# Retention gates evacuated without Silu into four buffers; Silu in place once the last head's exponentials are done, the gating products behind it

## The chip, the cores and the metric

The kernel runs on 1 core of one Trainium2 chip. The metric is the device time of one execution in microseconds (us), the median over several runs; smaller is better. A profiled execution gives the rows that are read here. Engines are called by their names or by the profile's: PE is TensorE (PEld its weight load), DVE VectorE, ACT ScalarE, POOL GpSimd, SP SyncE.

## The reference, cut to what matters

A model of three blocks on 256 tokens of width 1024: a differential attention and an mLSTM, each followed by a squared-ReLU MLP, and then a hybrid layer with a retention branch, a multi-head latent attention (MLA) branch, a third MLP and a gated embedding. The change is in the hybrid layer's two branches, which are computed side by side:

```python
h = rms_norm(x, norm_mix)
rq, rk, rv, rg, cq, ckv, krope, gr, gm = jnp.split(h @ w_in, offsets, axis=-1)
...
ro = retention(rq, rk, rv)                       # 4 heads of 512
ro = rms_norm(ro, ret_norm)
a_ret = (ro * jax.nn.silu(rg)) @ w_br            # rg: the retention gates, 2048 wide
...
s = q @ k * scale                                # MLA, 8 heads
s = jnp.where(causal, s, -1e30)
mo = jax.nn.softmax(s, axis=-1) @ v
a_mla = mo @ w_bm
mixed = jax.nn.sigmoid(gr) * a_ret + jax.nn.sigmoid(gm) * a_mla
```

## The kernel before, in words

**Weights in units.** Every product with a weight matrix is a `dense` group of 512 output columns. Its weights come in units of 128x1024 floats (512 KB) through a ring of 8: SyncE loads `raw`, ScalarE copies it, rounded, to `w_hi` (line 1190), VectorE subtracts it to get the rest, `w_lo` (line 1625), and TensorE makes three products for each pair of operands (lines 697 to 699). ScalarE and VectorE work 6 units ahead of TensorE. When TensorE has used a unit, `unit_used` counts up and the next load can start.

**Groups and banks.** The groups alternate between two pairs of PSUM banks, `pair0` and `pair1`. When a group is done ScalarE evacuates it (`empty`, line 1235), scaled by the rows' norm; the group after the next needs that evacuation. The order on every engine is written out by hand; the program's blocks for each engine list the groups in the same order, and the dictionary given to `dense` says what is done behind which unit of a group ("slot"). Nothing is reordered: an engine that waits holds everything behind it.

**The stretch of the change.** The groups `rv0` to `rv3` are the retention's values, with the retention's own products `ret0` to `ret3` between; `rg0` to `rg3` are the gates, and behind them come `gm0`, `gm1`, `gr0`, `gr1` (sigmoid gates) and `br0`, `br1`. Within `rg1` to `rg3` the slots run the MLA heads as a pipeline, `mla_slot(n)` behind one unit each: slots 0 to 3 in `rg1`, 4 to 7 in `rg2`, 8 and 9 behind the first two units of `rg3`. In slot n TensorE makes the scores of head n, the value product of head n-2 (lines 1079 to 1081), and the transpositions of head n-1's probabilities (line 725, out of `l_work`), which need that head's exponentials. VectorE masks the scores and takes the maxima (lines 2158 and 2161); ScalarE makes the exponentials (line 1494), copies the transposed probabilities back (line 1500) and scales head n-2's output (line 1507).

**The gates.** ScalarE evacuates gate group n with Silu into one of two buffers, `work[n % 2]`, which the retention's values used earlier. `gate_out(n)` on VectorE multiplies the retention's output, its norm factor and the gate (line 2096), two products of 128x512. `roT.0` to `roT.14` are the transpositions of that result in slots of `gm0` and `gm1`: ScalarE and VectorE split each into `b_hi` (line 1205) and `b_lo` (line 1643); `roT.0` and `roT.2` need product 0, `roT.4` and `roT.6` product 1, and so on.

**Tables.** Exp, Silu and Sigmoid are evaluated from different tables here. Where an activation needs another table than the one that is active, an ACT_TABLE_LOAD stands before it in the program, at the line of that activation. Copy and Square never have one.

Of the kernel before, what the change touches and what calls it, by code (L numbers as in the profile page):

```python
# [12 lines left out]
ALU = mybir.AluOpType  # L13
ACT = mybir.ActivationFunctionType
# [4 lines left out]
TT = S // P  # L19
# [3 lines left out]
HALF = 512  # L23
# [249 lines left out]
def build(nc, w, out):  # L273
    groups, group_list, stream, mlps = schedule(w)
# [4 lines left out]
    with ExitStack() as ctx:  # L279
        def sb(name, shape, dt=F32, scope=ctx):  # L280
            return scope.enter_context(nc.sbuf_tensor(name, [P, *shape], dt))

        def sem(name):
            return ctx.enter_context(nc.semaphore(name))
# [105 lines left out]
        ph = ctx  # L390
# [3 lines left out]
        work = sb("work", [2, TT, HALF], scope=ph)  # L394
# [30 lines left out]
        with ExitStack() as ph:  # L425
            kv = sb("kv", [TT, MLA_H, NOPE + P], scope=ph)
            lq_n = sb("lq_n", [MLA_H, S], scope=ph)
            lq_t = sb("lq_t", [MLA_H // 2, S], scope=ph)
            lk_n = sb("lk_n", [MLA_H, S], scope=ph)
            lk_t = sb("lk_t", [MLA_H // 2, S], scope=ph)  # L430
            l_work = sb("l_work", [2048], scope=ph)
        lk_flat = lk_n[:, :, :].rearrange("p h s -> p (h s)")
        rot = l_work[:, 0:TT * MLA_H * ROPE].rearrange("p (t h d) -> p t h d", t=TT, h=MLA_H)
        prod = l_work[:, 1024:2048].rearrange("p (t h d) -> p t h d", t=TT, h=MLA_H)
        l_e = l_work[:, 0:2 * SCORE].rearrange("p (b n) -> p b n", b=2)
        l_pt = l_work[:, 2 * SCORE:4 * SCORE].rearrange("p (b n) -> p b n", b=2)
        with ExitStack() as ph:
# [17 lines left out]
        group_act = sem("group_act")  # L455
# [70 lines left out]
        ret_out = sem("ret_out")  # L526
# [9 lines left out]
        l_exped = sem("l_exped")  # L536
        l_reced = sem("l_reced")
        gated = sem("gated")
        mixed = sem("mixed")
        p_loaded = sem("p_loaded")  # L540
        out_ready = sem("out_ready")
# [30 lines left out]
        def wait_group(eng, name):  # L572

            eng.wait_ge(unit_used, groups[name]["units"][-1][0] + 1)

        def group_ps(name):
            return pair[groups[name]["index"] % 2]
# [32 lines left out]
        def run_group(name, each, slots=None, part=slice(None)):  # L610

            for n, unit in list(enumerate(groups[name]["units"]))[part]:
                each(unit)
                if slots and n in slots:
                    slots[n]()
# [553 lines left out]
        def _(act):  # L1169
# [22 lines left out]
            def split_until(k):  # L1192

                while split_to[0] <= min(k, total_units - 1):
                    split_unit(split_to[0])
                    split_to[0] += 1

            def split_turn(name):

                wait_turn(act, name)  # L1200
                for src, hi, _, scale in split_parts(name):
                    if scale is None:
                        act.activation(hi, src, ACT.Copy).then_inc(turn_act, 1)
                    else:
                        act.activation(hi, src, ACT.Copy, scale=scale).then_inc(turn_act, 1)
# [16 lines left out]
            def dense(name, slots=None, part=slice(None), ahead=AHEAD):  # L1222

                run_group(name, lambda u: split_until(u[0] + ahead), slots, part)

            def empty(name, outs, func=ACT.Copy, scales=None):

                wait_group(act, name)
                for tt in range(TT):
                    ps = group_ps(name)[:, tt, 0:groups[name]["ncols"]]  # L1230
                    ps = ps if len(outs[tt].shape) == 2 else ps.rearrange("p (a b) -> p a b", a=outs[tt].shape[1])
                    if scales is None:
                        act.activation(outs[tt], ps, func).then_inc(group_act, 1)
                    else:
                        act.activation(outs[tt], ps, func, scale=scales[tt]).then_inc(group_act, 1)  # L1235

            def row_norm(v):
                return [rstd[:, v, tt:tt + 1] for tt in range(TT)]
# [251 lines left out]
            def mla_exp(h):  # L1490
                act.wait_ge(l_maxed, h + 1)
                b = h % 2
                for j, cols in enumerate((WIDE, TALL)):
                    last = act.activation(l_e[:, b, cols], l_e[:, b, cols], ACT.Exp, bias=l_nm[:, b, j:j + 1],
                                          accum_out=l_sum[:, b, j:j + 1])
                last.then_inc(l_exped, 1)

            def mla_probs(h):
                wait_turn(act, f"lp{h}")
                act.activation(l_pt[:, h % 2, :], turn_bank(f"lp{h}")[:, 0:SCORE], ACT.Copy).then_inc(turn_act, 1)  # L1500

            def mla_value(h):

                wait_turn(act, f"lv{h}")
                act.wait_ge(l_reced, h + 1)
                for tt in range(TT):
                    act.activation(lo_sb[:, tt, h * P:(h + 1) * P], turn_bank(f"lv{h}")[:, tt * P:(tt + 1) * P],
                                   ACT.Copy, scale=l_rec[:, h % 2, 1 - tt:2 - tt]).then_inc(turn_act, 1)

            def mla_slot(n):  # L1510
                if 1 <= n <= MLA_H:
                    mla_exp(n - 1)
                if n >= 2:
                    mla_value(n - 2)
                if 1 <= n <= MLA_H:
                    mla_probs(n - 1)
# [26 lines left out]
                    wait_turn(act, "rk1b")  # L1543
                empty(f"rv{n}", [work[:, n % 2, tt, :] for tt in range(TT)], scales=row_norm(5))

            def empty_gate(n):

                act.wait_ge(ret_out, 3 if n == 0 else 4)
                if n >= 2:
                    act.wait_ge(gated, n - 1)  # L1550
                empty(f"rg{n}", [work[:, n % 2, tt, :] for tt in range(TT)], ACT.Silu, row_norm(5))

            dense("rv0")
            empty_value(0)
# [9 lines left out]
            ret_squares(2)  # L1564
            dense("rg0")
            empty_gate(0)
            ret_squares(3)
            dense("rg1", {n: (lambda n=n: mla_slot(n)) for n in range(4)})
            empty_gate(1)
            dense("rg2", {n: (lambda n=n: mla_slot(4 + n)) for n in range(4)})  # L1570
            empty_gate(2)
            dense("rg3", {0: lambda: mla_slot(8), 1: lambda: mla_slot(9)})
            empty_gate(3)
            dense("gm0", {n: (lambda n=n: split_turn(f"roT.{2 * n}")) for n in range(4)})
            empty("gm0", [gm[:, tt, 0:HALF] for tt in range(TT)], ACT.Sigmoid, row_norm(5))
            dense("gm1", {n: (lambda n=n: split_turn(f"roT.{8 + 2 * n}")) for n in range(4)})
# [39 lines left out]
        def _(dve):  # L1616
# [11 lines left out]
            def split_until(k):  # L1628
                while split_to[0] <= min(k, total_units - 1):
                    split_unit(split_to[0])  # L1630
                    split_to[0] += 1

            def dense(name, slots=None, part=slice(None), ahead=AHEAD):
                run_group(name, lambda u: split_until(u[0] + ahead), slots, part)

            def split_turn(name):

                dve.wait_ge(turn_act, turn[name]["act_end"])
                for src, hi, lo, scale in split_parts(name):
                    if scale is None:  # L1640
                        dve.tensor_tensor(lo, src, hi, ALU.subtract).then_inc(turn_dve, 1)  # L1641
                    else:
                        dve.scalar_tensor_tensor(lo, src, scale, hi.bitcast(F32), ALU.mult, ALU.subtract)\
                            .then_inc(turn_dve, 1)
# [444 lines left out]
            def gate_out(n):  # L2089

                dve.wait_ge(ret_norm, 1)
                dve.wait_ge(group_act, groups[f"rg{n}"]["act_end"])
                dve.wait_ge(group_dve, groups["ret3"]["dve_end"])
                cols = slice(n * HALF, (n + 1) * HALF)
                for tt in range(TT):
                    last = dve.scalar_tensor_tensor(ret[:, tt, cols], ret[:, tt, cols], ret_r[:, tt, n:n + 1],
                                                    work[:, n % 2, tt, :], ALU.mult, ALU.mult)
                last.then_inc(gated, 1)

            def mla_sums_q():  # L2100
# [69 lines left out]
            def mla_slot(n):  # L2170
                if n < MLA_H:
                    mla_logits(n)
                if 1 <= n <= MLA_H:
                    mla_recip(n - 1)
# [31 lines left out]
            dense("rg0", {n: (lambda n=n: mla_rot_copy("mk", n)) for n in range(2)})  # L2206
            ret_value(3)
            dense("rg1", {n: (lambda n=n: mla_slot(n)) for n in range(4)})
            gate_out(0)
            dense("rg2", {n: (lambda n=n: mla_slot(4 + n)) for n in range(4)})  # L2210
            gate_out(1)
            dense("rg3", {0: lambda: mla_slot(8)})
            gate_out(2)
            gate_out(3)
            dense("gm0", {n: (lambda n=n: split_turn(f"roT.{2 * n}")) for n in range(4)})
            dense("gm1", {n: (lambda n=n: split_turn(f"roT.{8 + 2 * n}")) for n in range(4)})
            dense("gr0")
            dense("gr1")
# [209 lines left out]
```

## Time and profile before

| | |
|---|---|
| time of the runs | 1213.6, 1214.57, 1215.23 us; median 1214.57 |
| the profiled execution's own time | 1209.92 us |
| its span, first to last instruction | 1208.1 us |
| mean granted TensorE clock | 0.993 |
| TensorE busy | 1170.8 us, 97% |
| TensorE weight load busy | 965.5 us, 80% |
| VectorE busy | 748.1 us, 62% |
| ScalarE busy | 628.5 us, 52% |
| DMA, mean | 170 GB/s |

The profile shows one execution. A row of a timeline is one instruction (or several of one kind, "x2", merged): its start in us from the span's start, its length in us, the engine, the line, the operation, what it writes and reads, and in brackets how long its engine stood idle before it and for whom. Matmuls are pipelined: one shown as 0.39 us long is followed by the next 0.23 us after its start, so starts are to be compared, not ends.

### The profile page before, as it was taken

Reading aid. Unit: us, or ns where it says so; the run is one execution under the profiler, and the core shown is the slowest. Engines: PE = TensorE matmul, PEld = TensorE weight load, DVE = VectorE, ACT = ScalarE, POOL = GpSimd, SP = SyncE. Lnnn points to the kernel's source line nnn. Section 1 sums busy time; section 2 is a strip of 40 time slices with the busy share of each in tenths; the row PEclk is TensorE's granted clock in tenths of the full one; section 3 lists DMA queues with packets and bytes.
Section 4 is the critical chain, followed back from the end, with each engine's and each line's share of the span. In section 5 each row is a group of like instructions: output and inputs, shape, how many; then the busy total and the mean of one; then the engine's idle time right before and its main releaser. Section 6 shows DMA issues by size and latency. Waiting matters only on the chain.

```text
span 1208.1 us, 15885 instructions
## 1 busy us (share of the span) xinstructions
PE 1170.8 (97%) x5722; PEld 965.5 (80%) x5722; DVE 748.1 (62%) x1003; ACT 628.5 (52%) x970; POOL 63.5 (5%) x77
## 2 busy tenths in 40 slices
PE   6999999999999999999989999998999999999997
PEld 4778788888878878888877887777888877888886
DVE  4687656646585665656568778444645666556564
ACT  5587545435457654435455455565744454444443
POOL 2001000000000100000030042000000000000000
PEclk9999999999999999999999999999999999999999
DMA  8743455555456455555565555423665645555542
GB/s 248 257 145 122 156 177 190 191 191 189 143 141 172 150 181 191 188 182 187 168 190 182 168 162 157 139 88 88 174 182 184 190 150 176 190 191 191 191 160 85
DMA packets 95122, 205.60 MB, mean 170 GB/s; under 512 B 7805, under 2 KB 10149, under 8 KB 95072
## 3 DMA queue, kind: packets, MB, share of 16 engines
q1 hardware_dynamic: 93216, 199.61, 51.9%
q0 software_dynamic: 1696, 5.26, 1.5%
q8 instruction: 30, 0.49, 0.2%
q14 instruction: 20, 0.16, 0.0%
q10 hardware_dynamic: 160, 0.07, 0.0%
HBM read 203.86 MB, written 2.63 MB: 171 GB/s over the span
## 4 chain that ended last, share of the span: by engine, by line
PE 89%; DVE 3%; DMA 3%; ACT 3%; SPq 1%; issue 1%; POOL 0%; ACTq 0%
PE pair L697 16%; PE pair L699 16%; PE pair L698 16%; PE turn_ps L794 7%; PE pair L794 7%; PE turn_ps L796 4%; PE score L699 4%; PE score L697 4%; PE score L698 4%; PE pair L796 4%; PE turn_ps L725 3%; DMA raw<-in_w_in 1%; DVE w_lo L1625 1%; DMA raw<-in_attn_w_in 1%; SPq L644 1%
## 5 line engine op out<-in xcount | busy, mean ns | idle before, releaser
L1625 DVE TENSOR_TENSOR w_lo<-raw,w_hi 128x1024 fp32r<-128x1024 f32 (+2 forms) x381 | 457.6, 1224 | 199.5 <-ACT w_hi L1190 193.9
L1190 ACT ACTIVATE w_hi<-raw 128x1024 fp32r<-128x1024 f32 (+2 forms) x381 | 391.4, 1048 | 229.1 <-DMA raw<-in_mlp_w 63.2
L697 PE MATMUL pair<-w_hi,a_both 128*128 128x512 f32 (+3 forms) x560 | 226.1, 404 | 5.1 <-ACT lat_sb L1235 4.1
L699 PE MATMUL pair<-w_hi,a_both 128*128 128x512 f32 (+3 forms) x560 | 217.1, 388 | 0.0
L698 PE MATMUL pair<-w_lo,a_both 128*128 128x512 f32 (+3 forms) x560 | 216.5, 387 | 0.0
L794 PE MATMUL pair<-a_both,w_hi 128*128 128x512 f32 x384 | 143.5, 398 | 1.6 <-DVE up_sum L1671 1.6
L794 PE MATMUL turn_ps<-a_both,w_hi 128*128 128x512 f32 x384 | 142.6, 396 | 2.0 <-DVE p_lo L1641 2.0
L697 PEld LDWEIGHTS pair<-w_hi,a_both 128*128 128x128 f32 x560 | 107.1, 191 | 28.8 <-ACT lat_sb L1235 4.4
L699 PEld LDWEIGHTS pair<-w_hi,a_both 128*128 128x128 f32 x560 | 106.7, 191 | 21.8
L698 PEld LDWEIGHTS pair<-w_lo,a_both 128*128 128x128 f32 x560 | 107.3, 192 | 19.9 <-issue 1.2
L796 PE MATMUL pair<-a_both,w_lo 128*128 128x256 f32 x384 | 107.6, 280 | 0.0
L796 PE MATMUL turn_ps<-a_both,w_lo 128*128 128x256 f32 x384 | 107.5, 280 | 0.0
L1671 DVE TENSOR_TENSOR up_sum<-pair,up_low 128x512 f32<-128x512 f32 x24 | 16.6, 691 | 125.2 <-ACT up_low L1254 125.2
L794 PEld LDWEIGHTS pair<-a_both,w_hi 128*128 128x128 f32 x384 | 72.1, 188 | 20.5 <-DVE up_sum L1671 3.1
L794 PEld LDWEIGHTS turn_ps<-a_both,w_hi 128*128 128x128 f32 x384 | 72.0, 188 | 19.5 <-DVE p_lo L1641 2.3
L1254 ACT ACTIVATE up_low<-pair 128x512 f32<-128x512 f32 x24 | 14.3, 596 | 139.1 <-PE turn_ps L796 139.1
L796 PEld LDWEIGHTS pair<-a_both,w_lo 128*128 128x128 f32 x384 | 72.5, 189 | 0.9
L796 PEld LDWEIGHTS turn_ps<-a_both,w_lo 128*128 128x128 f32 x384 | 72.5, 189 | 0.0
L699 PE MATMUL score<-w_hi,h_lo 128*128 128x512 f32 x168 | 65.8, 392 | 0.0
L697 PE MATMUL pair<-w_hi,h_hi 128*128 128x512 f32 x168 | 65.8, 392 | 0.0
L699 PE MATMUL pair<-w_hi,h_lo 128*128 128x512 f32 x168 | 65.8, 392 | 0.0
L697 PE MATMUL score<-w_hi,h_hi 128*128 128x512 f32 x168 | 65.8, 391 | 0.0
(358 smaller groups left out, 1629.5 us busy)
## 6 DMA issues: line engine op xcount, KB each, us to landing
raw<-in_mlp_w SPq DMA_DIRECT2D x128, 512.0 KB, 3.3
raw<-in_w_in SPq DMA_DIRECT2D x64, 512.0 KB, 3.7
raw<-in_w_up SPq DMA_DIRECT2D x32, 512.0 KB, 3.5
raw<-in_w_down SPq DMA_DIRECT2D x32, 512.0 KB, 3.2
raw<-in_attn_w_in SPq DMA_DIRECT2D x24, 512.0 KB, 7.0
raw<-in_mlstm_w_in SPq DMA_DIRECT2D x24, 512.0 KB, 3.8
raw<-in_w_br SPq DMA_DIRECT2D x16, 512.0 KB, 3.7
raw<-in_attn_w_out SPq DMA_DIRECT2D x8, 512.0 KB, 3.7
```

The source lines that it names most:

```text
L644: sp.dma_start(dst, src).then_inc(landed[k % RING], 16)
L697: pe.matmul(o, hi, whi, start=start, stop=False)
L698: pe.matmul(o, hi, wlo, start=False, stop=False)
L699: return pe.matmul(o, lo, whi, start=False, stop=stop)
L725: last = pe.transpose(bank[:, j * P:(j + 1) * P], src, ident)
L794: pe.matmul(ups[i][:, b, :], w_hi[:, slot, cols], a_both[:, c, :, :], start=c == 0, stop=False)
L796: last = pe.matmul(ups[i][:, b, S:], w_lo[:, slot, cols], a_hi[:, c, :], start=False, stop=c == DC - 1)
L1190: act.activation(w_hi[:, k % RING, 0:n], raw[:, k % RING, 0:n], ACT.Copy).then_inc(hi_ready, 1)
L1254: act.activation(up_low[:, 2 * i:2 * i + 2, :], ups[i][:, :, S:], ACT.Copy).then_inc(up_copied, 1)
L1625: dve.tensor_tensor(w_lo[:, k % RING, 0:n], raw[:, k % RING, 0:n], w_hi[:, k % RING, 0:n], ALU.subtract).then_inc(lo_ready, 1)
L1671: dve.tensor_tensor(up_sum[:, 2 * i:2 * i + 2, :], ups[i][:, :, 0:S], up_low[:, 2 * i:2 * i + 2, :], ALU.add)\
```

## The change

The gate groups are evacuated by Copy in place of Silu, except the last, and into four buffers: a new tile `gate_raw` holds gates 0 and 1, `work` gates 2 and 3. Silu is then applied in place by a new function `silu_gate`: for gate 0 behind the third unit of `rg3`, for gate 1 behind the fourth, for gate 2 behind the group; head 7's exponentials are over by then. `gate_out` waits for a new semaphore `gate_silu`. On VectorE the products for gates 0 and 1 move from behind `rg1` and `rg2` to slots 2 and 3 of `rg3`, those for gates 2 and 3 from behind `rg3` to slots 0 and 1 of `gm0`, each behind the split of a transposition. The evacuations of gates 0 and 1 no longer wait for `ret_out`, the one of gate 2 waits for `ret_out` of 3 in place of 4, and none waits for `gated`.

```diff
@@ tiles, semaphores
+            gate_raw = sb("gate_raw", [2, TT, HALF], scope=ph)
+        gates = [gate_raw[:, n, :, :] for n in range(2)] + [work[:, n, :, :] for n in range(2)]
+        gate_silu = sem("gate_silu")
@@ ScalarE
-            def empty_gate(n):
-
-                act.wait_ge(ret_out, 3 if n == 0 else 4)
+            def empty_gate(n, func=ACT.Copy):
+
                 if n >= 2:
-                    act.wait_ge(gated, n - 1)
-                empty(f"rg{n}", [work[:, n % 2, tt, :] for tt in range(TT)], ACT.Silu, row_norm(5))
+                    act.wait_ge(ret_out, n + 1)
+                empty(f"rg{n}", [gates[n][:, tt, :] for tt in range(TT)], func, row_norm(5))
+
+            def silu_gate(n):
+
+                act.wait_ge(group_act, groups[f"rg{n}"]["act_end"])
+                act.activation(gates[n], gates[n], ACT.Silu).then_inc(gate_silu, 1)
@@
             empty_gate(2)
-            dense("rg3", {0: lambda: mla_slot(8), 1: lambda: mla_slot(9)})
-            empty_gate(3)
+            dense("rg3", {0: lambda: mla_slot(8), 1: lambda: mla_slot(9), 2: lambda: silu_gate(0),
+                          3: lambda: silu_gate(1)})
+            silu_gate(2)
+            empty_gate(3, ACT.Silu)
@@ VectorE
                 dve.wait_ge(ret_norm, 1)
-                dve.wait_ge(group_act, groups[f"rg{n}"]["act_end"])
+                if n < 3:
+                    dve.wait_ge(gate_silu, n + 1)
+                else:
+                    dve.wait_ge(group_act, groups["rg3"]["act_end"])
...
                     last = dve.scalar_tensor_tensor(ret[:, tt, cols], ret[:, tt, cols], ret_r[:, tt, n:n + 1],
-                                                    work[:, n % 2, tt, :], ALU.mult, ALU.mult)
+                                                    gates[n][:, tt, :], ALU.mult, ALU.mult)
@@
             dense("rg1", {n: (lambda n=n: mla_slot(n)) for n in range(4)})
-            gate_out(0)
             dense("rg2", {n: (lambda n=n: mla_slot(4 + n)) for n in range(4)})
-            gate_out(1)
-            dense("rg3", {0: lambda: mla_slot(8)})
-            gate_out(2)
-            gate_out(3)
-            dense("gm0", {n: (lambda n=n: split_turn(f"roT.{2 * n}")) for n in range(4)})
+            dense("rg3", {0: lambda: mla_slot(8), 2: lambda: gate_out(0), 3: lambda: gate_out(1)})
+            dense("gm0", {0: lambda: (split_turn("roT.0"), gate_out(2)), 1: lambda: (split_turn("roT.2"), gate_out(3)),
+                          2: lambda: split_turn("roT.4"), 3: lambda: split_turn("roT.6")})
```

The first place is ScalarE at the end of `rg1` (slot 3 ends with the copy to `l_work`). `l_work` of line 1494 is head 3's exponentials, `w_hi` the weight half six units ahead; behind "waits" stand the semaphores. Before:

```order
L1500 ACTIVATE l_work<-turn_ps 128x384 [waits turn_filled]
L1235 ACT_TABLE_LOAD [waits unit_used]
L1235 ACTIVATE work<-pair,rstd 128x512 [waits ret_out]
L1235 ACTIVATE work<-pair,rstd 128x512
L1190 ACTIVATE w_hi<-raw 128x1024 [waits landed1,unit_used]
L1494 ACT_TABLE_LOAD
L1494 ACTIVATE l_work,l_sum<-l_work,l_nm 128x256 [waits l_maxed]
L1494 ACTIVATE l_work,l_sum<-l_work,l_nm 128x128
```

The same place in the changed kernel, whose lines have moved down by three:

```order
L1503 ACTIVATE l_work<-turn_ps 128x384 [waits turn_filled]
L1238 ACTIVATE gate_raw<-pair,rstd 128x512 [waits unit_used]
L1238 ACTIVATE gate_raw<-pair,rstd 128x512
L1193 ACTIVATE w_hi<-raw 128x1024 [waits landed1,unit_used]
L1497 ACTIVATE l_work,l_sum<-l_work,l_nm 128x256 [waits l_maxed]
L1497 ACTIVATE l_work,l_sum<-l_work,l_nm 128x128
```

Both table loads are gone. It is the same at the end of `rg2`; at `rg0` the load ahead of the evacuation is gone, and the one ahead of head 0's exponentials is still there.

The second place is ScalarE in `rg3`, from the second to last weight half of the group on. Before:

```order
L1190 ACTIVATE w_hi<-raw 128x1024 [waits landed7,unit_used]
L1190 ACTIVATE w_hi<-raw 128x1024 [waits landed0,unit_used]
L1235 ACT_TABLE_LOAD [waits unit_used,gated]
L1235 ACTIVATE work<-pair,rstd 128x512 [waits ret_out]
L1235 ACTIVATE work<-pair,rstd 128x512
L1190 ACTIVATE w_hi<-raw 128x1024 [waits landed1,unit_used]
```

And in the changed kernel:

```order
L1193 ACTIVATE w_hi<-raw 128x1024 [waits landed7,unit_used]
L1558 ACT_TABLE_LOAD
L1558 ACTIVATE gate_raw<-gate_raw 128x1024 [waits group_act]
L1193 ACTIVATE w_hi<-raw 128x1024 [waits landed0,unit_used]
L1558 ACTIVATE gate_raw<-gate_raw 128x1024 [waits group_act]
L1558 ACTIVATE work<-work 128x1024 [waits group_act]
L1238 ACTIVATE work<-pair,rstd 128x512 [waits unit_used,ret_out]
L1238 ACTIVATE work<-pair,rstd 128x512
L1193 ACTIVATE w_hi<-raw 128x1024 [waits landed1,unit_used]
```

The table load has moved ahead by one weight half, and three Silus in place have come in.

The third place is VectorE from the last head's reciprocal to the splits in `gm0` (`ret` is the product of `gate_out`, `b_lo` the split of a transposition). Before:

```order
L2168 RECIPROCAL l_rec<-l_sum 128x2 [waits turn_act,l_exped]
L1625 TENSOR_TENSOR w_lo<-raw,w_hi 128x1024 [waits hi_ready] x3
L2096 SCALAR_TENSOR_TENSOR ret<-ret,ret_r,work 128x512 [waits group_dve,group_act,ret_norm]
L2096 SCALAR_TENSOR_TENSOR ret<-ret,ret_r,work 128x512
L2096 SCALAR_TENSOR_TENSOR ret<-ret,ret_r,work 128x512 [waits group_dve,group_act,ret_norm]
L2096 SCALAR_TENSOR_TENSOR ret<-ret,ret_r,work 128x512
L1625 TENSOR_TENSOR w_lo<-raw,w_hi 128x1024 [waits hi_ready]
L1643 SCALAR_TENSOR_TENSOR b_lo<-turn_ps,gains,b_hi 128x256 [waits turn_act]
```

And in the changed kernel:

```order
L2180 RECIPROCAL l_rec<-l_sum 128x2 [waits turn_act,l_exped]
L1634 TENSOR_TENSOR w_lo<-raw,w_hi 128x1024 [waits hi_ready] x2
L2108 SCALAR_TENSOR_TENSOR ret<-ret,ret_r,gate_raw 128x512 [waits group_dve,gate_silu,ret_norm]
L2108 SCALAR_TENSOR_TENSOR ret<-ret,ret_r,gate_raw 128x512
L1634 TENSOR_TENSOR w_lo<-raw,w_hi 128x1024 [waits hi_ready]
L2108 SCALAR_TENSOR_TENSOR ret<-ret,ret_r,gate_raw 128x512 [waits group_dve,gate_silu,ret_norm]
L2108 SCALAR_TENSOR_TENSOR ret<-ret,ret_r,gate_raw 128x512
L1634 TENSOR_TENSOR w_lo<-raw,w_hi 128x1024 [waits hi_ready]
L1652 SCALAR_TENSOR_TENSOR b_lo<-turn_ps,gains,b_hi 128x256 [waits turn_act]
L1652 SCALAR_TENSOR_TENSOR b_lo<-turn_ps,gains,b_hi 128x256
L2108 SCALAR_TENSOR_TENSOR ret<-ret,ret_r,work 128x512 [waits group_dve,gate_silu,ret_norm]
L2108 SCALAR_TENSOR_TENSOR ret<-ret,ret_r,work 128x512
```

Products 0 and 1, formerly in the MLA's slots, now stand in `rg3` a weight half apart, product 2 behind the first `b_lo`, and product 3, not shown, behind the second.

## Rows read from the trace of the kernel before

**Rows 1.** The page: the span, and TensorE's busy time, share and instructions.

```profile
span 1208.1 us, 15885 instructions
PE 1170.8 (97%) x5722; PEld 965.5 (80%) x5722; DVE 748.1 (62%) x1003; ACT 628.5 (52%) x970; POOL 63.5 (5%) x77
```

**Rows 2.** Waits of PE, 0 to 850 us: total us, times, longest us.

```profile
PE turn_ps L725 <- ACT l_work L1494: 4.3, 2, 3.2
```

**Rows 3.** Waits of PE from 850 us on, the first of four.

```profile
PE turn_ps L794 <- DVE p_lo L1641: 2.0, 1, 2.0
...
```

**Rows 4.** Timeline of PE, 804 to 818 us (slots 3 and 4).

```profile
...
806.14 0.39 PE L1081 MATMUL turn_ps<-kv,l_work 128*128 128x128 f32 x2
806.36 0.49 PE L725 MATMUL turn_ps<-square,l_work 128*128 128x128 f32 x3
...
811.97 0.39 PE L1081 MATMUL turn_ps<-kv,l_work 128*128 128x128 f32 x2
813.44 0.55 PE L725 MATMUL turn_ps<-square,l_work 128*128 128x128 f32 x3 [1.08 <-ACT l_work L1494]
...
```

**Rows 5.** Timeline of PE, 829 to 866 us (slot 8).

```profile
...
834.54 0.39 PE L1081 MATMUL turn_ps<-kv,l_work 128*128 128x128 f32 x2
838.10 0.55 PE L725 MATMUL turn_ps<-square,l_work 128*128 128x128 f32 x3 [3.17 <-ACT l_work L1494]
...
```

**Rows 6.** Timeline of PE behind `ret2` and behind `ret3`.

```profile
...
769.34 1.02 PE L1045 MATMUL pair<-work,ret_s 128*128 128x512 f32 x2
...
770.44 0.39 PE L698 MATMUL pair<-w_lo,a_both 128*128 128x512 f32 x1
...
783.81 1.02 PE L1045 MATMUL pair<-work,ret_s 128*128 128x512 f32 x2
...
785.29 0.40 PE L698 MATMUL pair<-w_lo,a_both 128*128 128x512 f32 x1
...
```

**Rows 7.** Timeline of ACT around the evacuations of `rg1` and `rg2`.

```profile
...
795.59 1.05 ACT L1190 ACTIVATE w_hi<-raw 128x1024 fp32r<-128x1024 f32 x1
796.53 0.50 ACT L1494 ACTIVATE l_work<-l_work,l_nm 128x256 f32<-128x256 f32 x1
...
807.59 1.28 ACT L1235 ACT_TABLE_LOAD   x1
...
810.04 1.05 ACT L1190 ACTIVATE w_hi<-raw 128x1024 fp32r<-128x1024 f32 x1
...
812.40 0.51 ACT L1494 ACTIVATE l_work<-l_work,l_nm 128x256 f32<-128x256 f32 x1
...
837.06 0.51 ACT L1494 ACTIVATE l_work<-l_work,l_nm 128x256 f32<-128x256 f32 x1
...
```

**Rows 8.** Table loads of ACT by line, 740 to 1000 us: busy us, mean ns.

```profile
L1235 ACT ACT_TABLE_LOAD x5 | 6.4, 1283 | 2.7 <-PE pair L699 2.6
...
L1494 ACT ACT_TABLE_LOAD x3 | 3.8, 1283 | 0.1
...
```

**Rows 9.** Timeline of DVE: head 7's maxima, and the products of gate 2.

```profile
...
830.95 0.61 DVE L2161 TENSOR_REDUCE l_nm<-l_work 128x1 f32<-128x256 f32 x2
...
847.39 1.41 DVE L2096 SCALAR_TENSOR_TENSOR ret<-ret,ret_r,work 128x512 f32<-128x512 f32 x2
...
```

**Rows 10.** Line 1411, the mLSTM's Silu in place: duration in ns, min/median/max.

```profile
L1411 ACT ACTIVATE ml_t<-ml_t x4: 617/620/632, 368.4 to 373.0; 128x512 f32<-128x512 f32 x4
```

**Rows 11.** Timeline of ACT in the second half of `rg3`.

```profile
...
842.64 1.06 ACT L1190 ACTIVATE w_hi<-raw 128x1024 fp32r<-128x1024 f32 x1
845.16 1.06 ACT L1190 ACTIVATE w_hi<-raw 128x1024 fp32r<-128x1024 f32 x1 [1.46 <-DMA raw<-in_w_in]
847.64 1.28 ACT L1235 ACT_TABLE_LOAD   x1 [1.43 <-PE pair L699]
...
```

**Rows 12.** Timeline of PE: the transpositions of `roT.0`.

```profile
...
850.11 0.60 PE L725 MATMUL turn_ps<-square,ret 128*128 128x128 f32 x4
...
```

**Rows 13.** Busy us (instructions) of each engine in 850 to 870 us; TensorE clock, DMA.

```profile
850.00:870.00 20.00, 20.00 (x103) 16.46 (x102) 14.64 (x21) 14.21 (x23) 0.00 (x0) 1.00 0.57 170
```

## The prediction

> **What bounds the kernel now.** I read the page first. TensorE has 1170.8 us of work in a span of 1208.1 us [rows 1], so the kernel is bound by TensorE's stream, and a change elsewhere is worth only what it takes out of TensorE's gaps, 37 us in all. Then I read TensorE's own waits. In the stretch with the gates the largest is 4.3 us in two pieces, the longer 3.2 us: the transpositions of line 725 waiting for the exponentials of line 1494 on ScalarE [rows 2]. The same query behind 850 us gives four waits, the longest of 2.0 us in the last MLP, and none of them is for a weight half (`w_hi`, `w_lo`) [rows 3]. So behind the gates TensorE is not short of weights, and microseconds won before stay won.
>
> Third, TensorE's timeline. In an undisturbed slot (slot 3) the last value product of line 1081 starts at 806.14 and the transpositions follow 0.22 us later. In slot 4 they start 1.47 us after line 1081 (811.97 to 813.44), in slot 8 3.56 us after it (834.54 to 838.10) [rows 4, 5]. Above the undisturbed 0.22 us the excess is **1.25 us** in slot 4 and **3.34 us** in slot 8. A third and smaller gap lies behind `ret3`: from the last line 1045 to the first line 698 of `rg1` there are 1.48 us (783.81 to 785.29), where the same place behind `ret2`, whose evacuation had no table load, took 1.10 us (769.34 to 770.44) [rows 6]. The excess is **0.38 us**.
>
> Fourth, ScalarE's timeline says why. At 807.59 it begins to evacuate `rg1`: a table load for Silu, two activations, a weight half at 810.04, another load, and only at 812.40 the exponential of head 3, for which TensorE's transpositions of slot 4 stand waiting [rows 7]. The same sequence for `rg2` ends with the exponential of head 7 at 837.06, and the transpositions of slot 8 start 1.04 us later [rows 5, 7].
>
> **What the change removes.** ScalarE's order of before has eight table loads in this stretch (five of line 1235, three of line 1494, each 1283 ns) [rows 8]. In the changed order `rg0` to `rg2` are evacuated by Copy, in whatever table is there (the `w_hi` copies between exponentials already run so), and three loads are left: for head 0's exponential, for the first Silu, for `gm0`'s Sigmoid. Five go.
>
> What a load costs ScalarE is read from two pairs. Weight half to exponential without a load: 795.59 to 796.53, 0.94 us. With one: 810.04 to 812.40, 2.36 us [rows 7]. The difference is 1.42 us: the load, and the overlap of 0.13 us that back-to-back activations have and a load breaks. The page "ScalarE: Activation LUTs" of the Trainium skill, section "What ACT_TABLE_LOAD costs", gives about 1.28 us for the load and about 1.38 us more for a drain, 2.66 us a switch. This trace agrees with the load and not with the drain; by the page's figure the slot 8 gap would vanish wholly, and the sum below would be 5.0 instead of 4.5 us.
>
> Now each gap:
> - `rg1` (behind `ret3`): its first matmul needs `rg0` evacuated. The load at the head of that evacuation goes, 1.42 us against a lateness of 0.38 us. All of it goes: **0.38 us**.
> - Slot 4: two loads ahead of the exponential of head 3, 2.84 us, against an excess of 1.25 us. The exponential would start at 812.40 − 2.84 = 809.56 and be over some 1.6 us before TensorE has finished line 1081. All goes: **1.25 us**.
> - Slot 8: two loads ahead of the exponential of head 7, which would start at 837.06 − 2.84 = 834.22. Is it ready by then? Its maxima on VectorE start at 830.95 and last 0.61 us, so yes [rows 9]. The transpositions follow 1.04 us behind, at 835.26, where TensorE could take them at 834.76. Of 3.34 us **2.84 us** go and 0.50 us stay, since the evacuation of `rg2` and the weight half still stand ahead of the exponential.
>
> Sum: 0.38 + 1.25 + 2.84 = 4.47, **4.5 us**.
>
> **What it adds.** Three Silus in place of 128x1024 on ScalarE. The nearest row is the Silu in place of 128x512 at 617 to 632 ns [rows 10]; the `w_hi` copy of 128x1024, a double width, takes 1.06 us [rows 11]. I take 1.05 us each, 3.2 us together (bounds: 0.62 us if width cost nothing, 1.26 us for twice the narrow row). They lie where ScalarE has room. In the frame of before: weight half at 842.64 for 1.06 us, then idle 1.46 us to the next at 845.16, and idle 1.43 us again until TensorE finishes `rg3` and the load starts at 847.64 [rows 11]. With the change: load 843.7 to 845.0, Silu 0 to 846.05, weight half to 847.0, Silu 1 to 848.0, Silu 2 to 849.0, then `rg3`'s evacuation. Before, that evacuation's activations started behind their load, at 847.64 + 1.28 = 848.9. So the three Silus cost nothing there; without that cover they would cost ScalarE 3.2 us, and even so `rg3`'s pair of banks is next wanted by `gm1`, four units later.
>
> **Where the new wait goes.** `gate_out(0)` now waits for Silu 0 and its two products take 1.41 us [rows 9]: done at about 847.6. TensorE wants it at 850.11, for `roT.0` [rows 12]: 2.5 us of slack. Queued behind it on VectorE is one `w_lo`, for a unit six ahead. Products 2 and 3 go in between the `b_lo` splits of `gm0`. VectorE is busy 14.64 of 20 us there, the last product of before included [rows 13]; one pair more leaves about 4 us idle, and products 2 and 3 are wanted by `roT.8` and `roT.12`, units later. Taking the two products out of slots 4 and 7 frees VectorE 2.8 us, which nobody waited for. Nothing is issued anew on the DMA queues, and no step is moved past one. The removed waits on `gated` and `ret_out` had been met long before.
>
> **From the profile to the median.** The sum is made in the profiled execution, 1209.92 us with its 1208.1 us span. The median of the runs is 1214.57 us, 4.65 us above that; the gaps are waits between engines, so I take 4.5 us off each: 1205.4 us for a profiled execution like this one, 1210.1 us for the median, 0.37% less.
>
> **The rivals.**
> - *Forecast: the three gaps shrink as computed.* 1210.1 us, own range 1209.3 to 1211.2 (a spread of the runs of ±0.8 us; the slot 8 term between one load's 1.42 and the whole 3.34 us). Chance 0.72.
> - *The whole slot 8 gap goes.* That needs the two loads to hold the chain for 3.34 us, 1.67 us each, against 1.42 us by my pair. It gives 0.38 + 1.25 + 3.34 = 4.97, 1209.6 us. This is how it would come out by the page's 2.66 us a switch. Chance 0.08.
> - *Another wait takes the place in slot 8*, the longer gap: the weight half between `rg2`'s evacuation and the exponential then waits for its transfer or its ring slot, which the loads hide today. Only 1.63 us are won, 1212.9 us, within 0.2%. Against it: in the row of before that half starts without idle time, and its unit's slot has been free for units. The same number comes if some of the gain is given back later, against which stand the rows behind 850 us [rows 3]. Chance 0.15.
> - *Slower: TensorE waits at `roT.0` for product 0.* Place: between the first and second unit of `gm0`. Price: each microsecond by which the product ends more than 2.5 us after my 847.6. The kernel is slower than before once it is 2.5 + 4.5 = 7.0 us late, and by over 0.2% from 9.4 us. At 12 us late it is 1210.1 + 9.5 = 1219.6 us. Three Silus of 1.05 us can't do that; they would have to take some 4 us each, or Silu 0 would have to be held by a weight half that arrives late. Chance 0.05.
>
> **How the numbers follow.** A change of 0.2%, 2.4 us, is about what a measurement of this kernel can tell from none. The first two cases are faster by more (0.80, of which I give 0.02 to the spread of the runs, and take 0.03 from the third case, where half the slot 8 term may come): faster 0.81. Same: 0.14. Slower: 0.05. The range reaches from under the second case, 1209.6 less the spread of 0.8 (1208.8, taken to 1208.5), to the third, 1212.9.
>
> **What would show it.** In the changed kernel's trace: three table loads between 770 and 865 us where there were eight; slot 4's transpositions directly behind line 1081 (0.22 us); slot 8's 0.7 us behind it, TensorE's wait for the exponentials down from 4.3 to about 0.5 us; no wait of TensorE for `ret` ahead of `roT.0`; three Silus of about 1.05 us in `rg3`, the first product done some 2.5 us before TensorE's transposition. The prediction is wrong if a wait for `w_lo`, for a turn's bank or for `ret` stands in TensorE's list, or if the exponential of head 7 still starts more than 3 us behind the start of `rg2`'s evacuation.

## The result, and the profile after

The changed kernel took **1206.93 us** (median of 20 runs, 1202.99 to 1212.3). The kernel before took 1212.66 us (20 runs, 1209.68 to 1218.45; the three runs behind the 1214.57 us in the table above are among them). The medians are 5.7 us apart; the ratio is 0.9949, 95% interval 0.9935 to 0.9963, which is 6.2 us faster (4.5 to 7.9). Faster was forecast; the time forecast, 1210.1 us, is 3.2 us too high, and 1206.93 lies below the range of 1208.5 to 1212.9.

The profiled execution of the changed kernel is one of the longest of the 20, 1211.89 us. Its span is longer than the span before (mean granted clock 0.989 against 0.993, and a long wait near the start), so here the two totals say nothing. The page, and TensorE's waits from 0 to 850 us (total us, times, longest us):

```profile
span 1210.1 us, 15878 instructions
PE 1175.0 (97%) x5719; PEld 970.4 (80%) x5722; DVE 747.7 (62%) x1003; ACT 624.5 (52%) x968; POOL 63.4 (5%) x77
```

```profile
...
PE score L904 <- DVE da_e L1812: 4.7, 1, 4.7
...
PE turn_ps L728 <- ACT l_work L1497: 0.3, 1, 0.3
```

The 4.7 us are a wait in the first block, far from the change, for an operation that TensorE did not wait for in the execution of before; the last experiment comes back to it. The wait for the exponentials has gone from 4.3 us to 0.3 [rows 2]. Of the eight table loads between 740 and 1000 us [rows 8] three are left, as forecast:

```profile
...
L1497 ACT ACT_TABLE_LOAD x1 | 1.3, 1283 | 0.0
L1558 ACT ACT_TABLE_LOAD x1 | 1.3, 1283 | 0.0
L1238 ACT ACT_TABLE_LOAD x1 | 1.3, 1283 | 0.0
```

TensorE's timeline of the changed kernel answers to [rows 4 to 6] and [rows 12] (line numbers are higher by three):

```profile
...
776.01 1.02 PE L1048 MATMUL pair<-work,ret_s 128*128 128x512 f32 x2
...
777.11 0.39 PE L701 MATMUL pair<-w_lo,a_both 128*128 128x512 f32 x1
...
790.48 1.02 PE L1048 MATMUL pair<-work,ret_s 128*128 128x512 f32 x2
...
791.57 0.40 PE L701 MATMUL pair<-w_lo,a_both 128*128 128x512 f32 x1
...
818.25 0.39 PE L1084 MATMUL turn_ps<-kv,l_work 128*128 128x128 f32 x2
818.48 0.49 PE L728 MATMUL turn_ps<-square,l_work 128*128 128x128 f32 x3
...
839.50 0.39 PE L1084 MATMUL turn_ps<-kv,l_work 128*128 128x128 f32 x2
840.21 0.55 PE L728 MATMUL turn_ps<-square,l_work 128*128 128x128 f32 x3 [0.32 <-ACT l_work L1497]
...
852.22 0.60 PE L728 MATMUL turn_ps<-square,ret 128*128 128x128 f32 x4
...
```

Behind `ret3` 1.09 us in place of 1.48, as behind `ret2`. Slot 4: 0.23 in place of 1.47. Slot 8: 0.71 in place of 3.56. Nothing is idle ahead of `roT.0`.

ScalarE's timeline, at the end of `rg1` and in `rg3`, answers to [rows 7] and [rows 11]:

```profile
...
813.73 1.28 ACT L1238 ACTIVATE gate_raw<-pair,rstd 128x512 f32<-128x512 f32 x2
814.88 1.08 ACT L1193 ACTIVATE w_hi<-raw 128x1024 fp32r<-128x1024 f32 x1
815.82 0.53 ACT L1497 ACTIVATE l_work<-l_work,l_nm 128x256 f32<-128x256 f32 x1
...
845.83 1.28 ACT L1558 ACT_TABLE_LOAD   x1
847.12 1.06 ACT L1558 ACTIVATE gate_raw<-gate_raw 128x1024 f32<-128x1024 f32 x1
848.09 1.05 ACT L1193 ACTIVATE w_hi<-raw 128x1024 fp32r<-128x1024 f32 x1
849.04 1.04 ACT L1558 ACTIVATE gate_raw<-gate_raw 128x1024 f32<-128x1024 f32 x1
849.99 1.04 ACT L1558 ACTIVATE work<-work 128x1024 f32<-128x1024 f32 x1
850.94 1.24 ACT L1238 ACTIVATE work<-pair,rstd 128x512 f32<-128x512 f32 x2
...
```

Weight half to exponential is 0.94 us without the load, as the undisturbed pair of [rows 7] said. The Silus take 1.04 to 1.06 us each. VectorE's timeline has product 0, and its busy time in 850 to 870 us answers to [rows 13]:

```profile
...
848.28 1.42 DVE L2108 SCALAR_TENSOR_TENSOR ret<-ret,ret_r,gate_raw 128x512 f32<-128x512 f32 x2 [1.21 <-ACT gate_raw L1558]
...
```

```profile
850.00:870.00 20.00, 20.00 (x101) 16.47 (x100) 15.76 (x24) 15.45 (x26) 0.00 (x0) 1.00 0.57 162
```

Product 0 is done at 849.70, 2.5 us ahead of `roT.0`. TensorE stays busy for the whole of the 20 us.

To compare executions whose starts differ, the document measures **the stretch**: from the first matmul of `ret2` (line 1043 of before, 1046 of the changed kernel) to the first transposition of `roT.0`. Its start, before and after:

```profile
...
767.62 1.02 PE L1043 MATMUL pair<-work,ret_s 128*128 128x512 f32 x2
...
```

```profile
...
774.29 1.02 PE L1046 MATMUL pair<-work,ret_s 128*128 128x512 f32 x2
...
```

Before it runs from 767.62 to 850.11, 82.49 us; after, from 774.29 to 852.22, 77.93 us. The change takes 4.56 us out of it; the sum said 4.47. So the time came from where the prediction looked for it, but the runs gained more than the stretch shows. What the further 1.6 us are is the question of the experiments.

### The profile page after: what moved, and what is told of

Read it like the earlier page. It is cut to its first block, busy times and chain, and to the rows that moved or that the text cites. A ratio compares the mean times of both kernels' runs of the same rounds, so it can differ in the third digit from the quotient of the medians.

```text
span 1210.1 us, 15878 instructions
## 1 busy us (share of the span) xinstructions
PE 1175.0 (97%) x5719; PEld 970.4 (80%) x5722; DVE 747.7 (62%) x1003; ACT 624.5 (52%) x968; POOL 63.4 (5%) x77
## 4 chain that ended last, share of the span: by engine, by line
PE 89%; DMA 4%; DVE 3%; ACT 2%; issue 1%; POOL 1%; SPq 0%; ACTq 0%
PE pair L700 16%; PE pair L702 16%; PE pair L701 16%; PE turn_ps L797 7%; PE pair L797 7%; PE turn_ps L799 4%; PE score L702 4%; PE score L701 4%; PE score L700 4%; PE pair L799 4%; PE turn_ps L728 3%; DMA raw<-in_attn_w_in 1%; DVE w_lo L1634 1%; DMA bias<-bias_replicas 1%; DMA bias_replicas<-bias_scratch 1%; PE score L1071 1%
## 5 line engine op out<-in xcount | busy, mean ns | idle before, releaser
L700 PEld LDWEIGHTS pair<-w_hi,a_both 128*128 128x128 f32 x560 | 108.8, 194 | 28.2 <-ACT lat_sb L1238 4.7
L702 PEld LDWEIGHTS pair<-w_hi,a_both 128*128 128x128 f32 x560 | 108.5, 194 | 21.9
L701 PE MATMUL pair<-w_lo,h_hi 128*128 128x512 f32 x168 | 65.8, 392 | 0.0
L701 PE MATMUL score<-w_lo,h_hi 128*128 128x512 f32 x168 | 65.8, 392 | 0.0
```

What stands on the lines that cost most here:

```text
L700: pe.matmul(o, hi, whi, start=start, stop=False)
L701: pe.matmul(o, hi, wlo, start=False, stop=False)
L702: return pe.matmul(o, lo, whi, start=False, stop=stop)
```

## The experiments

The theory: the change acts through the table loads ahead of TensorE's waits and nothing else. The rivals: part of the gain comes from where tiles and instructions now lie; or the gaps cost more than their length. From e1 on each kernel was timed against the kernel before in the same session. There were two sessions; in the first (e1 to e4) the kernel before had a median of 1212.57 us over 35 runs, in the second (f1 to f4) of 1213.99 us.

| kernel | stretch, us | gap in slots 4, 8 | median, us | ratio to before, 95% |
|---|---|---|---|---|
| before | 767.62 to 850.11: 82.49 | 1.47, 3.56 | 1212.66 | |
| changed | 774.29 to 852.22: 77.93 | 0.23, 0.71 | 1206.93 | 0.9949 (0.9935 to 0.9963) |
| e1, four buffers alone | 770.78 to 853.26: 82.48 | 1.47, 3.56 | 1212.3 | 0.9999 (0.9983 to 1.0016) |
| e2, no Silu | 770.12 to 848.04: 77.92 | 0.23, 0.71 | 1206.24 | 0.995 (0.9936 to 0.9965) |
| e3, exponentials first | 772.72 to 850.09: 77.37 | 0.22, 0.22 | 1207.91 | 0.9965 (0.9951 to 0.998) |
| e4, Silu of gate 2 back | 767.77 to 850.14: 82.37 | 0.23, 3.55 | 1211.38 | 0.9988 (0.9972 to 1.0004) |
| f1, before again | 768.33 to 852.36: 84.03 | 1.47, 3.56 | 1212.91 | 0.9989 (0.997 to 1.0009) |
| f2, changed again | 771.56 to 849.48: 77.92 | 0.23, 0.71 | 1208.22 | 0.995 (0.9934 to 0.9967) |
| f3, slot 8's gap longer | 768.42 to 856.14: 87.72 | 1.47, 6.58 | 1216.16 | 1.0032 (1.0011 to 1.0054) |
| f4, product 0 late | 771.94 to 851.62: 79.68 | 0.23, 0.71 | 1211.25 | 0.9968 (0.9947 to 0.9988) |

A gap here is the time from the start of the last value product (line 1081 of before) to that of the transpositions.

**e1: the buffers without the rest.** Against the kernel before:

```diff
+            gate_raw = sb("gate_raw", [2, TT, HALF], scope=ph)
+        gates = [gate_raw[:, n, :, :] for n in range(2)] + [work[:, n, :, :] for n in range(2)]
+        gate_silu = sem("gate_silu")
-                empty(f"rg{n}", [work[:, n % 2, tt, :] for tt in range(TT)], ACT.Silu, row_norm(5))
+                empty(f"rg{n}", [gates[n][:, tt, :] for tt in range(TT)], ACT.Silu, row_norm(5))
-                                                    work[:, n % 2, tt, :], ALU.mult, ALU.mult)
+                                                    gates[n][:, tt, :], ALU.mult, ALU.mult)
```

> The kernel before with the new tile, the new semaphore and four gate buffers, but every gate still evacuated with Silu at its old place and every product where it was. Theory 1 (the change acts through the table loads in the gates' stretch alone, 4.5 us, and the rest of the measured 5.7 to 6.2 us is scatter of the runs): within 1 us of the kernel before, eight table loads, stretch from the first line of ret2 to the transpositions of roT.0 of 82.5 us as before. Theory 2 (1.5 to 2 us of the gain are real and lie outside that stretch, from where tiles and instructions lie): 1.5 to 2 us faster than before with the stretch still at 82.5 us.

The stretch is 82.48 us, with eight table loads, and the ratio 0.9999. No gain from the place of the tiles is seen. The interval alone, which reaches down to 0.9983 or 2.1 us faster, would still allow the 1.5 us of theory 2; e2 speaks against it, since it gains as much as the changed kernel without the new tile. The buffers are only what lets Silu be put off.

**e2: the Silu left out, nothing else.**

```diff
-                empty(f"rg{n}", [work[:, n % 2, tt, :] for tt in range(TT)], ACT.Silu, row_norm(5))
+                empty(f"rg{n}", [work[:, n % 2, tt, :] for tt in range(TT)], ACT.Copy, row_norm(5))
```

> The kernel before with one word changed: the gates are evacuated by Copy, so Silu is left out of the computation; buffers, waits and products as before. Table loads 8 to 2. Theory 1: the stretch falls from 82.5 to 77.9 us as in the changed kernel, and the time by 4.5 us. Theory 2: the same stretch, but only 4.5 us of the changed kernel's 5.7 to 6.2. Rival to both (the buffers or the moved products carry the gain): the stretch stays above 79 us, since work[0] and work[1] still serve two gates each.

Two table loads are left. One word gives the changed kernel's stretch to 0.01 us, with the products in their old places. TensorE's timeline in slot 8 of this kernel:

```profile
...
835.33 0.39 PE L1081 MATMUL turn_ps<-kv,l_work 128*128 128x128 f32 x2
836.04 0.55 PE L725 MATMUL turn_ps<-square,l_work 128*128 128x128 f32 x3 [0.32 <-ACT l_work L1494]
...
```

The activations themselves are no shorter: the two that evacuate `rg1` take 1.26 us with Silu (808.88 in before) and 1.28 with Copy (813.73 above). So the loads carry the stretch's whole gain, and the three Silus in place and the moved products cost nothing: this kernel has neither and is no faster. The runs, too, gained as much as with the change, 0.50%, and again more than the stretch's 4.57 us, which are 0.38%.

**e3: the exponentials ahead of the evacuations.** Against the changed kernel:

```diff
-            empty_gate(1)
-            dense("rg2", {n: (lambda n=n: mla_slot(4 + n)) for n in range(4)})
-            empty_gate(2)
-            dense("rg3", {0: lambda: mla_slot(8), ...
+            dense("rg2", {n: (lambda n=n: (mla_slot(4 + n), empty_gate(1) if n == 0 else None)) for n in range(4)})
+            dense("rg3", {0: lambda: (mla_slot(8), empty_gate(2)), ...
```

> The changed kernel with the evacuations of rg1 and rg2 moved behind slots 4 and 8 on ScalarE, so that the exponentials of heads 3 and 7 stand ahead of them. By my account of slot 8 (0.5 us left because the evacuation and a weight half stand ahead of the exponential) the transpositions follow the last value product after 0.22 us in place of 0.71, and the kernel is 0.5 us faster than the changed one, 5.0 us faster than before in the stretch. If the leftover has another cause it stays at 0.7 us.

The timeline of TensorE in slot 8:

```profile
...
837.92 0.39 PE L1084 MATMUL turn_ps<-kv,l_work 128*128 128x128 f32 x2
838.14 0.49 PE L728 MATMUL turn_ps<-square,l_work 128*128 128x128 f32 x3
...
```

The leftover gap is closed, as reckoned: the stretch is 0.56 us shorter than the changed kernel's. The runs can't show half a microsecond: 1207.91 us is no less than the changed kernel's.

**e4: two of the loads back.** Against the changed kernel, gate 2 alone is evacuated with Silu at the end of `rg2`:

```diff
-            empty_gate(2)
+            empty_gate(2, ACT.Silu)
...
-            silu_gate(2)
```

> The changed kernel with gate 2 alone evacuated with Silu at its old place, which brings back two table loads ahead of head 7's exponential. By my 1.42 us a load slot 8's gap grows by 2.84 us, to 3.5 us, and 2.8 of the 4.5 us are given back: 1.7 us faster than before in the stretch. By a load of 2.66 us the gap would grow by 5.3 us, to 6 us.

The gap grew from 0.71 to 3.55 us, 2.84 us for two loads, 1.42 us each to the hundredth. But the stretch grew by 4.44 us, to 82.37. The further 1.6 us stand behind the gap. TensorE's timeline there, then the windows around it; columns are the window, its length, busy us (instructions) of PE, PEld, DVE, ACT and POOL, then the granted share of TensorE's clock (1.00 is 2.4 GHz, 0.50 is 1.2 GHz), the DMA's busy share and GB/s:

```profile
...
832.98 0.39 PE L1084 MATMUL turn_ps<-kv,l_work 128*128 128x128 f32 x2
836.53 0.81 PE L728 MATMUL turn_ps<-square,l_work 128*128 128x128 f32 x3 [3.17 <-ACT l_work L1497]
...
```

```profile
832.00:836.50 4.50, 1.36 (x10) 1.05 (x8) 1.23 (x1) 4.47 (x9) 0.00 (x0) 1.00 0.39 117
836.50:840.00 3.50, 3.47 (x10) 2.88 (x11) 1.32 (x2) 1.92 (x4) 0.00 (x0) 0.53 0.00 0
```

Behind the gap the granted clock is 0.53, nearly all of it at the lower level of 1.2 GHz, and TensorE gets 10 matmuls done in 3.5 us. The kernel before and e1, in their profiled executions, have no such fall of the clock behind the same gap (first before, then e1):

```profile
838.00:841.00 3.00, 2.90 (x14) 2.46 (x15) 1.01 (x2) 1.99 (x5) 0.00 (x0) 1.00 0.00 0
```

```profile
841.00:844.00 3.00, 2.74 (x14) 2.31 (x15) 0.85 (x2) 2.15 (x6) 0.00 (x0) 1.00 0.00 0
```

In the runs e4 is 1.5 us faster than before (from 0.5 slower to 3.4 faster), near the 1.7 expected. That gives a new theory 2: the gap also costs clock, in a part of the executions. It was put to f1 and f3.

**f1 and f2: before and after once more**, without an edit.

> The kernel before, unchanged. My account so far: in the stretch from ret2 to roT.0 it takes 82.5 us at the full clock; where TensorE's granted clock falls to half right behind slot 8's gap (as in the kernel with the Silu of gate 2 back at its old place) it takes about 1.7 us more. Theory 1 (the change removes 4.5 us of waits and nothing else): 82.5 us, no half clock between 830 and 850 us. Theory 2 (the gap also costs clock in a part of the executions): 84.2 us here, or 82.5 with the fall in other executions.

> The changed kernel, unchanged. Both theories: 77.9 us in the stretch, no half clock between 830 and 850 us. For the time: 0.4 to 0.6% below before.

This time the kernel before shows it. TensorE in slot 8, and the window behind:

```profile
...
835.25 0.39 PE L1081 MATMUL turn_ps<-kv,l_work 128*128 128x128 f32 x2
838.81 0.90 PE L725 MATMUL turn_ps<-square,l_work 128*128 128x128 f32 x3 [3.17 <-ACT l_work L1494]
...
```

```profile
839.00:842.00 3.00, 3.00 (x9) 2.49 (x9) 0.79 (x1) 1.69 (x4) 0.00 (x0) 0.50 0.00 0
...
```

The same program, the same gap of 3.56 us, and a stretch of 84.03 us where the first profile had 82.49: 1.54 us for a clock of 0.50 behind the gap. The first profile was an execution without the fall. The changed kernel repeats its 77.9 us (77.93, 77.92) and shows none.

**f3: the gap made longer.** Against the kernel before, two activations of one column, whose result nobody reads, force two more loads:

```diff
             empty_gate(2)
+            act.activation(lam_e[:, 0:1], lam_s[:, 0:1], ACT.Exp)
+            act.activation(lam_e[:, 1:2], lam_s[:, 1:2], ACT.Silu)
```

> The kernel before with two more table loads ahead of head 7's exponential, each forced by an activation of one column that nobody reads. Theory 1: slot 8's gap grows from 3.56 to about 6.8 us (two loads of 1.42 us and two small activations of 0.2 us), and the kernel is 3.2 us slower than before, no more. Theory 2: the longer gap brings the fall of the clock behind it more often, so that the time grows by up to 5 us, and the trace shows half clock behind slot 8.

```profile
835.34 0.39 PE L1081 MATMUL turn_ps<-kv,l_work 128*128 128x128 f32 x2
...
841.92 0.90 PE L725 MATMUL turn_ps<-square,l_work 128*128 128x128 f32 x3 [6.19 <-ACT l_work L1494]
...
```

```profile
833.00:840.00 7.00, 2.73 (x16) 2.18 (x14) 1.14 (x3) 6.91 (x10) 0.00 (x0) 1.00 0.27 75
840.00:846.00 6.00, 4.08 (x11) 3.34 (x12) 2.22 (x3) 3.79 (x9) 0.00 (x0) 0.50 0.00 0
```

The gap grew by 3.02 us, the stretch by 5.23. The 2.2 us above the gap's own growth are the clock at 0.50, which here was down already in the gap's last two microseconds, before TensorE started again at 841.92. In the runs it is 0.32% slower than before, 3.9 us (1.3 to 6.6), between theory 1's 3.2 and theory 2's 5: they allow both, the trace shows the second.

**f4: product 0 late.** Against the changed kernel, four copies in place ahead of Silu 0:

```diff
+                for _ in range(4 if n == 0 else 0):
+                    mark(act.activation(gates[n], gates[n], ACT.Copy))
+                    own()
                 act.activation(gates[n], gates[n], ACT.Silu).then_inc(gate_silu, 1)
```

> The changed kernel with four copies in place, each waiting for the one before, ahead of Silu 0, which makes Silu 0 and product 0 about 4.4 us late. By my slack of 2.5 us TensorE then waits 1.9 us at roT.0, and the kernel is 1.9 us slower than the changed one. If product 0 were not what roT.0 waits for, or ScalarE's added work itself were the cost, the wait would be 0 or 4.4 us.

On ScalarE the copies take 4.34 us, on TensorE `roT.0` waits:

```profile
...
843.34 4.34 ACT L1559 ACTIVATE gate_raw<-gate_raw 128x1024 f32<-128x1024 f32 x4
847.70 1.28 ACT L1561 ACT_TABLE_LOAD   x1
...
```

```profile
851.62 0.66 PE L728 MATMUL turn_ps<-square,ret 128*128 128x128 f32 x4 [1.62 <-DVE ret L2111]
...
```

The stretch is 1.75 us longer than the changed kernel's (1.9 expected): 4.3 us of delay less 2.5 us of slack, the wait being for product 0. The work on ScalarE itself cost nothing beyond that. In the same session f4 took 1211.25 us and the changed kernel 1208.22; the two intervals overlap, so the runs do not tell 3.0 us from 1.75.

**The clock in all runs.** The span and the mean granted clock are known for each single run (of the kernel before, for the two sessions' 35 runs each). The span times (1 - clock) is about what the lower level took; the remainder is about what the span would be at the full clock. It is an estimate, since idle time at the lower level is counted as well. The means, with standard errors of 0.2 to 0.6 us for the remainder and 0.3 to 0.8 for what the clock took:

| kernel | runs | remainder, us | taken by the lower clock, us |
|---|---|---|---|
| changed | 20 | 1194.8 | 10.1 |
| before, first session | 35 | 1199.3 | 11.8 |
| e1 | 12 | 1199.6 | 11.3 |
| e2 | 12 | 1194.4 | 10.2 |
| e3 | 12 | 1194.0 | 12.1 |
| e4 | 12 | 1197.4 | 12.2 |
| before, second session | 35 | 1199.7 | 12.3 |
| f1, before again | 12 | 1199.6 | 11.7 |
| f2, changed again | 12 | 1195.2 | 10.9 |
| f3 | 12 | 1201.3 | 13.7 |
| f4 | 12 | 1197.5 | 10.9 |

The remainder falls by 4.9 us in e2 and 4.5 in f2, which is the stretch's 4.56 within the error. What the runs gained above it, 1.6 and 1.4 us, is lower clock. Where in the kernel it was saved a mean cannot say. Over all, the clock took 11.9 us in the 106 runs with a gap of about 3.56 us in slot 8 and 10.8 in the 68 runs with at most 0.71 (1.2 us apart, standard error 0.3), but e3, without a gap, stands at 12.1.

**The wait near the start.** The changed kernel, e3, f2 and f4 all have the wait of the first block, 2.7 to 4.7 us long in one piece, and in all four the granted clock is down around it (0.66 to 0.83 in 55 to 65 us). The other six traces have at most 2.4 us there and 1.00. In the changed kernel's trace:

```profile
...
59.42 1.23 PE L904 MATMUL score<-da_k,da_q 64*128 64x256 f32 x4 [4.71 <-DVE da_e L1812]
...
```

```profile
55.00:65.00 10.00, 5.58 (x20) 4.30 (x20) 9.93 (x17) 5.62 (x15) 0.00 (x0) 0.66 0.17 60
```

So a second place in the same kernels shows a wait followed by a fall of the clock. Whether the change brings the longer wait, and how, is open; it would work against the gain, and the remainders above show no loss of its size over the runs.

## Why the prediction was right in its working and wrong in its number

**The three gaps: right.** `rg1` 0.38 us (measured 1.48 to 1.09), slot 4 1.25 us (1.47 to 0.23), slot 8 2.84 us of 3.34 with 0.50 left (3.56 to 0.71). Sum 4.47, the stretch says 4.56. e2 shows that the loads alone do it, e4 that two loads in slot 8 are worth 2.84 us, e3 that the 0.50 left are the evacuation ahead of the exponential (0.56 us less stretch without it).

**A load's price: right.** 1.42 us, from one pair of rows, holds in e4 (2.84 for two). The 2.66 us a switch of the Trainium skill's page "ScalarE: Activation LUTs" (section "What ACT_TABLE_LOAD costs") would have made slot 8's gap 6 us in e4. It was 3.55. The rival in which the whole gap goes is out too: in the changed kernel 0.49 us above the undisturbed 0.22 stayed.

**What is added: right.** Silus of 1.05 us, product 0 with 2.5 us to spare; f4 shows what happens when that is used up. The rival of another wait in slot 8 did not come, nor did the slower one.

**"From the profile to the median": wrong, twice.** The forecast is 3.2 us too high: 1.9 us are the base (1214.57 less 1212.66), 1.3 us the gain (the medians are 5.73 us apart, the sum was 4.47). The first failure is the base and the spread. The sum was taken off 1214.57 us, the median of three runs, with a spread of ±0.8 us read from these three. Over 20 runs the median of the kernel before is 1212.66, and they scatter from 1209.68 to 1218.45; that the three stood high was chance, that they were taken for the spread was not. Off 1212.66 the same sum gives 1208.2 us. The profile at hand could have warned: its own 1209.92 us lay 4.65 us under that median.

The second is the step "the gaps are waits between engines, so I take 4.5 us off each". The clock is a term that the sum put at nothing without a reason. The gap of slot 8 costs more than its length in those executions in which TensorE's clock falls with it: 1.54 us more in f1, 1.6 in e4, 2.2 in f3 with the longer gap. Of the five traces with a gap of 3.5 us or more in slot 8 three show the fall (e4, f1, f3) and two do not (before, e1); of the five with 0.2 to 0.7 us there (changed, e2, e3, f2, f4) none does. The profile of before happened to be one without. So in the stretch the change is worth 4.6 us against an execution without the fall and 6.1 us against one with it. The runs gave 6.2 us (4.5 to 7.9), and 6.1 both for e2 and for the changed kernel again; by the means of the runs the waits make 4.9 and 4.5 us of it and the lower clock 1.6 and 1.4.

**What stays open.** The runs show that there was less low clock after the change; that it was saved at slot 8 only the traces suggest. How often the clock falls there is not measured in the runs whose trace was not kept: if in half of them, as in two of the four traces with a gap of 3.56 us, the mean gain would be 5.3 us, and the remaining 0.8 us is within the interval; the 1.2 us over all runs would be three falls in four of 1.6 us, an estimate that puts the whole difference down to slot 8. e3, with no gap left and the shortest stretch, gained only 4.2 us (2.4 to 5.9). Its remainder is the lowest of all, 1194.0 us, but the lower clock took 12.1; why is not shown. And why the clock falls with the same gap in one execution and not in another is open.

## What to carry to other kernels

A table load is cheap where ScalarE is idle and dear where an exponential stands behind it for which TensorE waits: count the loads between the last wait that TensorE passes and the one it stops at, price them by a pair of rows with and without a load, and cap the gain by the gap. An extra buffer that lets a function be put off until the other table's work is over costs nothing if the in-place pass fits ScalarE's idle time ahead of its first reader. And a time in absolute microseconds needs more than three runs of base; where one profile shows a gap of several microseconds on TensorE, look at the granted clock behind it in a second profile, since a gap can cost more in one execution than in another. With span and mean clock of every run at hand, the gain can be split into waits and clock before a second cause is looked for.

## What the runs showed of the hardware that was not expected

The same program with the same gap of 3.56 us on TensorE kept its full granted clock behind it in one execution (1.00 in 838 to 841 us of before) and had the lower level in another (0.50 in 839 to 842 us of f1), which cost 1.54 us. Gaps of up to 0.71 us in slot 8 were followed by no fall in the five traces that have them, nor was f4's idle time of 1.62 us at `roT.0` in its one. In the first block TensorE's idle time of 2.75 us (f4) was enough for a fall and 2.36 us (f1) brought none, while in slot 8 two of four executions passed 3.17 us of idle time without one: in these traces the length of a gap alone does not say whether the clock falls.
